# RWKV-7 layers of a four-layer backbone: head-pair keys turned by block transposes and a DRAM exchange instead of identity products

## The chip, the cores and the metric

One core of a Trainium2 chip runs the whole program in one launch. The metric is the device time in microseconds, the median of the runs. The core has TensorE (PE, its weight loads are shown as PEld), VectorE (DVE), ScalarE (ACT), GpSimd (POOL) and SyncE (SP), and each goes through its own instruction list in order. They wait for one another on semaphores.

## The reference, cut to what matters

Four layers over 512 tokens (256 of context, 256 latent) of width 1024. Layers 0 and 3 mix tokens with a bidirectional RWKV-7 recurrence in 16 heads of 64. For each direction and head:

```python
def step(s, inp):
    r_t, w_t, k_t, v_t, kk_t, a_t = inp
    s_kk = jnp.einsum('bhvk,bhk->bhv', s, kk_t)
    s = (s * w_t[:, :, None, :] - s_kk[..., None] * (kk_t * a_t)[:, :, None, :]
         + v_t[..., None] * k_t[:, :, None, :])
    return s, jnp.einsum('bhvk,bhk->bhv', s, r_t)
```

`k_t` is the key that is added, `kk_t * a_t` the one that is taken off. The second direction is the same on flipped tokens, and the context's last state starts the latent part. Layer 1 is Mamba-2, layer 2 attention, and a gated ConvFFN stands after each. The last layer gives no output for the context.

## The kernel before, in words

All data is float32, channels on partitions and tokens along the free dimension, so that two heads fill the 128 partitions (`HALF` names the two halves of 64). The recurrence is done in chunks of 64 tokens (`Q`; there are `NQ` = 8), for eight pairs of heads `i` (`KD`), both directions `d`, written `q = 2 * i + d`.

**The chain.** For each chunk `c` of each `q` there are three dependent steps. W makes a right-hand side from values and state. ACT copies it from PSUM to `WS`. U multiplies by the chunk's inverse matrix `INV`, and DVE copies the result to `US`. S adds `BK` times values and `BK` times `US` to the state (`sp`), makes the outputs, and DVE scales the new state into `STR`. The two directions alternate: W0, W1, U0, U1, S0, S1.

**The work around it.** The order is written out by hand in `slot_steps(h)`. A pair of heads has two slots of 24 chain steps, and each slot has 25 places `k`. At a place the `early` steps are issued, then one chain step, then the `late` steps. Every engine walks the same list and does its own part of each step. While the chain of pair `i - 1` ends and that of pair `i` begins, the lists prepare pairs `i` and `i + 1`, in two halves `s` of four chunks: Gram matrices (`GT`, `R`, `H2`), the inverse (`IB`, `E`, then the levels `Z` and `X`), the decays and keys (`L01` to `sd1`) and the end of pair `i - 1` (`P1` to `P3`). `SD` holds the decayed keys to add, `ADS[i % 2]` those to remove.

**The keys by token.** The `sp` products need both key tensors with tokens on partitions. The step `HB` (`by_token`, four parts in each slot) gets them by multiplying every 64x64 block with the identity `id64` into PSUM bank 7. ACT copies the bank to `BK` (label `bk`).

**The inverse's way through DRAM.** For each half, ACT copies the Gram blocks out (label `n`), SP stores them (`grams_out`, L2499, after a wait at L2496), loads them in blocks of 16 (`blocks_in`, L2507), and POOL inverts them (`block_inverse`). SP stores the result (`inverse_out`, L2514) and loads it back (`inverse_in`, L2522), and DVE expands it at step `E` (`expand`: two products at L3158, transposes at L3162 and L3163). SP does this in order for half 0, then half 1 of each pair. Only the first inverse is DVE's.

Other lines that matter here: L2549 is the helper that issues all these matrix products, L2835 the one for ACT's copies, L3194 the copy to `US`, L3205 the new state, L2946 one ACT instruction of `P2` that comes once for each pair.

## Time and the profile before

| | us |
|---|---|
| median of 3 runs | 3613.45 (3612.48 to 3619.98) |
| the profiled execution | 3610.41 |
| its span, first to last instruction | 3608.6 |
| PE busy | 3447.1 (96%) |
| DVE busy | 2487.9 (69%) |
| ACT busy | 1156.4 (32%) |
| POOL busy | 590.4 (16%) |

The profile is of one execution. Times on rows are in microseconds from the span's start. Busy shares are averages over layers with different limits: the two stretches that the change touches are the chains of layer 0 (about 250 to 665) and of layer 3 (about 2960 to 3342). A matrix product of float32 appears as two records, and neighbouring records overlap, so the pace is read from the distance between starts and not from one record's length.

### The profile page before, as it was taken

Reading aid. Unit: us, or ns where it says so; the run is one execution under the profiler, and the core shown is the slowest. Engines: PE = TensorE matmul, PEld = TensorE weight load, DVE = VectorE, ACT = ScalarE, POOL = GpSimd, SP = SyncE. Lnnn points to the kernel's source line nnn. Section 1 sums busy time; section 2 is a strip of 40 time slices with the busy share of each in tenths; the row PEclk is TensorE's granted clock in tenths of the full one; section 3 lists DMA queues with packets and bytes.
Section 4 is the critical chain, followed back from the end, with each engine's and each line's share of the span. In section 5 each row is a group of like instructions: output and inputs, shape, how many; then the busy total and the mean of one; then the engine's idle time right before and its main releaser. Section 6 shows DMA issues by size and latency. Waiting matters only on the chain. (4 is left out here: it accounts for less than half of the span.)

```text
span 3608.6 us, 74335 instructions
## 1 busy us (share of the span) xinstructions
PE 3447.1 (96%) x28653; PEld 2513.5 (70%) x28653; DVE 2487.9 (69%) x4562; ACT 1156.4 (32%) x2482; POOL 590.4 (16%) x1128
## 2 busy tenths in 40 slices
PE   7998998999999999999999999999999997888999
PEld 2447777688786455555888876678877456777887
DVE  7986665489897657653898954469987956664431
ACT  4035554133202444431233014323310225663210
POOL 1015553000000323320000000000000105553000
PEclk9998999999999999999999999999999998999999
DMA  6641111244353323223444520043434541111454
GB/s 219 207 136 24 21 22 32 74 133 130 118 161 97 105 79 102 82 76 99 129 126 127 162 83 28 25 126 121 136 118 129 170 129 25 25 24 27 134 152 133
DMA packets 584315, 365.07 MB, mean 101 GB/s; under 512 B 126144, under 2 KB 553480, under 8 KB 581928
## 3 DMA queue, kind: packets, MB, share of 16 engines
q1 hardware_dynamic: 557544, 250.40, 25.1%
q0 software_dynamic: 26432, 110.07, 8.7%
q8 instruction: 223, 3.65, 0.4%
q14 instruction: 116, 0.95, 0.1%
HBM read 348.73 MB, written 11.67 MB: 100 GB/s over the span
## 5 line engine op out<-in xcount | busy, mean ns | idle before, releaser
L275 PE MATMUL PS<-H,WR 128*128 128x512 f32 (+1 forms) x1424 | 477.1, 494 | 0.0
L591 DVE SCALAR_TENSOR_TENSOR WORK<-WORK,SC 128x512 f32<-128x512 f32 x616 | 418.3, 746 | 0.7
L275 PEld LDWEIGHTS PS<-H,WR 128*128 128x128 f32 x1424 | 268.0, 190 | 187.3 <-issue 167.2
L2549 PE MATMUL PS<-WORK 64*64 64x64 f32 (+2 forms) x6944 | 361.0, 231 | 29.5 <-ACT BIG L2846 16.6
L571 POOL DMA_DIRECT2D WORK<-in_ada_w_dram x88 | 66.4, 755 | 1857.7 <-DVE WORK L591 839.6
L1474 PE MATMUL PS<-BIG,WR 128*128 128x512 f32 (+1 forms) x944 | 329.4, 503 | 5.2 <-DMA WR<-in_rw_wo_dram 1.7
L2549 PEld LDWEIGHTS PS<-WORK 64*64 64x64 f32 (+1 forms) x6944 | 282.1, 139 | 69.2 <-ACT WORK L2835 23.0
L1474 PEld LDWEIGHTS PS<-BIG,WR 128*128 128x128 f32 x944 | 175.7, 190 | 132.6 <-issue 111.8
L2835 ACT ACTIVATE WORK<-PS 128x64 f32<-128x64 f32 (+3 forms) x528 | 161.4, 326 | 292.0 <-PE PS L2549 286.7
L1012 ACT ACTIVATE WORK<-PS 128x512 f32<-128x512 f32 x252 | 134.7, 541 | 335.6 <-PE PS L945 285.1
L945 PE MATMUL PS<-BIG 128*128 128x256 f32 x984 | 223.9, 380 | 0.0
L275 PE MATMUL PS<-WORK,WR 128*128 128x512 f32 (+1 forms) x544 | 211.7, 545 | 0.9 <-DMA WR<-in_rw_wr_dram 0.9
L945 PEld LDWEIGHTS PS<-BIG 128*128 128x128 f32 x984 | 186.0, 190 | 25.1
L2549 PE MATMUL PS<-BIG,WORK 64*64 64x64 f32 x1920 | 145.7, 228 | 47.0 <-DVE WORK L3194 36.3
L945 PE MATMUL PS<-H,BIG 128*128 128x256 f32 x768 | 177.8, 380 | 0.6 <-ACT H L728 0.4
L945 PE MATMUL PS<-BIG,WORK 128*128 128x256 f32 x792 | 176.3, 379 | 0.0
L1093 DVE SCALAR_TENSOR_TENSOR WORK<-WORK,PV 128x510 f32<-128x510 f32 x252 | 171.7, 743 | 2.6 <-ACT WORK L1023 2.6
L275 PEld LDWEIGHTS PS<-WORK,WR 128*128 128x128 f32 x544 | 102.0, 190 | 101.0 <-issue 88.5
L945 PEld LDWEIGHTS PS<-BIG,WORK 128*128 128x128 f32 x792 | 150.5, 190 | 20.5
L945 PEld LDWEIGHTS PS<-H,BIG 128*128 128x128 f32 x768 | 145.2, 190 | 22.5 <-ACT H L728 3.0
L3009 POOL TENSOR_TENSOR BTN<-BTN,BTP 64x14 f32<-64x14 f32 (+1 forms) x420 | 149.8, 357 | 32.9
L2549 PEld LDWEIGHTS PS<-BIG,WORK 64*64 64x64 f32 x1920 | 100.6, 136 | 74.0 <-DVE WORK L3194 23.4
(363 smaller groups left out, 6391.0 us busy)
## 6 DMA issues: line engine op xcount, KB each, us to landing
WORK<-in_ada_w_dram POOLq DMA_DIRECT2D x88, 1024.0 KB, 6.3
WR<-in_ffn_w_in_dram SPq DMA_DIRECT2D x220, 256.0 KB, 2.9
BIG<-in_ffn_w_in_dram SPq DMA_DIRECT2D x132, 256.0 KB, 3.4
WR<-in_ffn_w_out_dram SPq DMA_DIRECT2D x106, 256.0 KB, 2.8
WR<-in_ssd_w_in_dram SPq DMA_DIRECT2D x96, 256.0 KB, 2.8
BIG<-scratch_dram POOLq DMA_DIRECT2D x8, 2048.0 KB, 7.9
BIG<-in_ffn_w_out_dram SPq DMA_DIRECT2D x36, 256.0 KB, 3.2
BIG<-in_ada_w_dram SPq DMA_DIRECT2D x4, 2048.0 KB, 15.5
```

What stands on the lines that cost most here:

```text
L275: mm = pe.matmul(outs, WR[:, slot, k, 0:m], rhs(k), start=first and k == 0, stop=last and k == nk - 1)
L571: pool.dma_start(AW[:, 2048 * h:2048 * h + 2048].rearrange("p (k c) -> p k c", k=4), rows(a["ada_w"][l])[:, 4 * h:4 * h + 4, n * 512:n * 5 ...
L591: lag(vec.scalar_tensor_tensor(ACC3[:, s_], w, by, ACC3[:, s_], ALU.mult, ALU.add), label)
L945: mm = pe.matmul(out, lhs(k), rhs(k), start=start and k == 0, stop=stop and k == 3)
L1012: s(act.activation(EV[f % 2][:, n0:n0 + n, :], ps[:, 0:n, :], ACT.Copy), lab(f, "e" + bank))
L1093: lag(vec.scalar_tensor_tensor(dst, whole[h][:, :, t // 2:SEG - 1 + t // 2], tap(t, h, f), dst, ALU.mult, ALU.add), lab(f, "cv") if (t, h) ...
L1474: mm = pe.matmul(PS[:, bank, lo:T], WR[:, opened[label], k, :], rhs(8 * r + k), start=r == 0 and k == 0, stop=last and k == nk - 1)
L2549: return pe.matmul(o, lhs, rhs, start=start, stop=stop)
L2835: s(act.activation(dst, src, ACT.Copy), f"{t}.{label}")
L3009: g(pool.tensor_tensor(below, below, product, ALU.add), f"{t}.t{i}.ib{s_}" if j_ == BLK - 2 else None)
```

## The change

The step `HB` is dropped on PE and ACT. A new step `TB` on DVE turns the keys in 32x32 blocks straight from `SD` and `ADS` into `BK`, one instruction for each half `s`, direction `d` and kind `n`, so eight for each pair. A 64x64 turn needs two of the 32-partition blocks exchanged as well. SP does that through a new DRAM tensor: four stores (`swap_out`) and four loads (`swap_in`) for each half, each of 32 partitions by 512 elements (64 KB). The new `BK` interleaves four chunks, so a chunk's keys are read by PE with a step of four elements. `E` and the levels `Z` and `X` move to later places. The copy to `US` of the second direction moves from DVE to ACT. Some waits change with that.

```diff
-        G2, BK, G1R = by_chunk(P), by_chunk(P), by_chunk(Q)
+        G2, G1R = by_chunk(P), by_chunk(Q)
+        BK = work(2 * NQ * P).rearrange("p (s d n a f) -> p s d n a f", s=2, d=2, n=2, a=2)
...
             if s == 0:
-                at = (4, 5, 7, 8, 10, 11, 13, 14) if i else (21, 21, 22, 22, 23, 23, 24, 24)
+                at = (8, 9, 11, 12, 14, 15, 17, 18) if i else (21, 21, 22, 22, 23, 23, 24, 24)
                 early += [(k, *step) for k, step in zip(at, levels)]
-                early += [(1 if i else 20, "E", i, 0), (0, "R", i, 0, 0), (2, "R", i, 0, 1), (9, "H2", both[0], 0),
-                          (12, "HB", both[0], 0, 0), (15, "HB", both[0], 0, 1), (16, "H2", both[1], 0),
-                          (18, "HB", both[1], 0, 0), (20, "HB", both[1], 0, 1)]
+                early += [(5 if i else 20, "E", i, 0), (0, "R", i, 0, 0), (2, "R", i, 0, 1), (9, "H2", both[0], 0),
+                          (16, "H2", both[1], 0)]
+                late += [(k, "TB", i, 0, d, n) for k, (d, n) in zip((0, 1, 2, 3), ((0, 1), (1, 1), (0, 0), (1, 0)))]
...
             else:
-                at = (5, 6, 8, 9, 12, 13, 15, 16)
+                at = (8, 9, 11, 12, 14, 15, 17, 18)
                 early += [(k, *step) for k, step in zip(at, levels)]
-                early += [(2, "E", i, 1), (14, "R", i, 1, 0), (17, "R", i, 1, 1), (2, "H2", both[0], 1),
-                          (3, "HB", both[0], 1, 0), (4, "HB", both[0], 1, 1), (7, "H2", both[1], 1),
-                          (10, "HB", both[1], 1, 0), (11, "HB", both[1], 1, 1)]
+                early += [(5, "E", i, 1), (14, "R", i, 1, 0), (17, "R", i, 1, 1), (2, "H2", both[0], 1),
+                          (7, "H2", both[1], 1)]
+                late += [(k, "TB", i, 1, d, n) for k, (d, n) in zip((0, 1, 4, 6), ((0, 1), (1, 1), (0, 0), (1, 0)))]
...
+            swap = swapped.rearrange("(s b p d n f) -> s b p d n f", s=2, b=4, p=32, d=2, n=2)
+            def swap_out(i, s_):
+                sp.wait_ge(vec_done, C.at(f"{t}.t{i}.tb{s_}"))
+                if i:
+                    sp.wait_ge(swap_loaded, C.at(f"{t}.t{i - 1}.bk{s_}"))
+                for b in range(4):
+                    sp.dma_start(swap[s_, b ^ 1], BK[32 * b:32 * b + 32, s_, :, :, 1 - b % 2, :]).then_inc(
+                        swap_stored, C.mark(swap_stored, f"{t}.t{i}.swap{s_}" if b == 3 else None, 16))
+            def swap_in(i, s_):
+                sp.wait_ge(swap_stored, C.at(f"{t}.t{i}.swap{s_}"))
+                for b in range(4):
+                    sp.dma_start(BK[32 * b:32 * b + 32, s_, :, :, 1 - b % 2, :], swap[s_, b]).then_inc(
+                        swap_loaded, C.mark(swap_loaded, f"{t}.t{i}.bk{s_}" if b == 3 else None, 16))
             for i in range(KD):
                 grams_out(i, 0)
                 blocks_in(i, 0)
                 if i == 0:
                     grams_out(i, 1)
                     blocks_in(i, 1)
+                else:
+                    swap_out(i - 1, 1)
+                    swap_in(i - 1, 1)
                 inverse_out(i, 0)
                 inverse_in(i, 0)
                 if i:
                     grams_out(i, 1)
                     blocks_in(i, 1)
+                swap_out(i, 0)
+                swap_in(i, 0)
                 inverse_out(i, 1)
                 inverse_in(i, 1)
+            swap_out(KD - 1, 1)
+            swap_in(KD - 1, 1)
...
             def vt(n):
-                pe.wait_ge(act_done, C.at(f"{t}.{2 * n - 1}.bk1") if n else C.at(f"{t}.t{n}.a1"))
+                pe.wait_ge(act_done, C.at(f"{t}.t{n}.a1"))
...
                 if c % 4 == 0:
-                    pe.wait_ge(act_done, C.at(f"{t}.{q}.bk{c // 4}"))
-                pe.wait_ge(vec_done, C.at(f"{t}.{q}.us{c}"))
+                    pe.wait_ge(swap_loaded, C.at(f"{t}.t{i}.bk{c // 4}"))
+                by_token = [BK[:, c // 4, d, n].rearrange("p a (f c) -> p (a f) c", c=4)[:, :, ch % 4] for n in range(2)]
+                pe.wait_ge(act_done if d else vec_done, C.at(f"{t}.{q}.us{c}"))
                 if c < NQ - 1:
                     for hs in HALF:
-                        mm(PS[hs, d, P:P + Q], BK[hs, d, c, Q:P], v_tok[hs, tok(ch)], stop=False)
+                        mm(PS[hs, d, P:P + Q], by_token[1][hs], v_tok[hs, tok(ch)], stop=False)
                     for hs in HALF:
-                        last = mm(PS[hs, d, P:P + Q], BK[hs, d, c, 0:Q], US[d][hs, :], start=False)
+                        last = mm(PS[hs, d, P:P + Q], by_token[0][hs], US[d][hs, :], start=False)
...
             def replacement(n, d):
                 act.wait_ge(vec_done, C.at(f"{t}.ka"))
                 if n:
-                    act.wait_ge(pe_done, C.at(f"{t}.{2 * n - 2 + d}.hb1"))
+                    act.wait_ge(pe_done, C.at(f"{t}.{2 * n - 2 + d}.h21"))
+                    act.wait_ge(vec_done, C.at(f"{t}.{2 * n - 2 + d}.turned1"))
...
+            def chain_u(q, c):
+                if q % 2:
+                    act.wait_ge(pe_done, C.at(f"{t}.{q}.u{c}"))
+                    copy(US[1], PS[:, 1, Q:P], f"{q}.us{c}")
...
+            def by_token(i, s_, d, n):
+                half, q = SEGS[s_], 2 * i + d
+                vec_last()
+                if i:
+                    vec.wait_ge(pe_done, C.at(f"{t}.{q - 2}.sp{min(4 * s_ + 3, NQ - 2)}"))
+                src = (SD if n else ADS[i % 2])[:, d, half].rearrange("p (c b t) -> p b c t", b=2, t=32)
+                dst = BK[:, s_, d, n].rearrange("p a (f c) -> p a c f", c=4)
+                lag(vec.transpose(dst, src), f"{t}.{q}.turned{s_}" if n else f"{t}.t{i}.tb{s_}" if d else None)
...
             def chain_u(q, c):
+                if q % 2:
+                    return
                 vec.wait_ge(pe_done, C.at(f"{t}.{q}.u{c}"))
-                lag(vec.tensor_copy(US[q % 2], PS[:, q % 2, Q:P]), f"{t}.{q}.us{c}")
+                lag(vec.tensor_copy(US[0], PS[:, 0, Q:P]), f"{t}.{q}.us{c}")
```

## Rows read from the trace of the kernel before

**Rows 1.** The page: span and PE's busy time.

```profile
span 3608.6 us, 74335 instructions
...
PE 3447.1 (96%) x28653; PEld 2513.5 (70%) x28653; DVE 2487.9 (69%) x4562; ACT 1156.4 (32%) x2482; POOL 590.4 (16%) x1128
```

**Rows 2.** Timeline of ACT, L2946, once a pair: start, length, idle before.

```profile
448.14 0.69 ACT L2946 ACTIVATE WORK<-PS,MC 128x512 f32<-128x512 f32 x1 [0.82 <-PE PS L2549]
...
495.25 0.69 ACT L2946 ACTIVATE WORK<-PS,MC 128x512 f32<-128x512 f32 x1 [0.82 <-PE PS L2549]
...
3149.28 0.47 ACT L2946 ACTIVATE WORK<-PS,MC 128x256 f32<-128x256 f32 x1 [0.40 <-PE PS L2549]
...
3192.46 0.47 ACT L2946 ACTIVATE WORK<-PS,MC 128x256 f32<-128x256 f32 x1 [0.40 <-PE PS L2549]
```

**Rows 3.** Windows, one pair of layer 0: busy by engine, clock, DMA share, GB/s.

```profile
454.00:501.00 47.00, 42.34 (x1104) 36.29 (x1104) 31.48 (x75) 27.74 (x67) 25.07 (x62) 1.00 0.14 23
```

**Rows 4.** Groups by form of PE from 200 to 700, those that read constants.

```profile
L2549 PE MATMUL PS<-K,BIG 64*64 64x64 f32 x1024 | 47.0, 224 | 1.2 <-ACT WORK L2835 1.2
...
L2549 PE MATMUL PS<-K,WORK 64*64 64x64 f32 x256 | 16.6, 218 | 0.0
```

**Rows 5.** Timeline of PE, layer 0, second half of one pair.

```profile
471.82 0.63 PE L2549 MATMUL PS<-K,BIG 64*64 64x64 f32 x16
...
475.87 0.63 PE L2549 MATMUL PS<-K,BIG 64*64 64x64 f32 x16
...
476.45 0.63 PE L2549 MATMUL PS<-K,BIG 64*64 64x64 f32 x16
478.75 0.33 PE L2549 MATMUL PS<-BIG,WORK 64*64 64x64 f32 x4 [1.67 <-DVE WORK L3194]
...
481.98 1.36 PE L2549 MATMUL PS<-WORK 64*64 64x32 f32 x40
483.15 0.66 PE L2549 MATMUL PS<-K,BIG 64*64 64x64 f32 x16
```

**Rows 6.** Timeline of DVE, layer 0, around both steps `E` of one pair.

```profile
454.16 0.45 DVE L3162 STREAM_TRANSPOSE WORK<-WORK 128x256 f32<-128x256 f32 x1
454.53 0.40 DVE L3163 STREAM_TRANSPOSE WORK<-WORK 128x256 f32<-128x256 f32 x1
455.88 0.23 DVE L3194 COPY WORK<-PS 128x64 f32<-128x64 f32 x1 [0.95 <-PE PS L2549]
...
461.59 0.28 DVE L3205 SCALAR_TENSOR_TENSOR WORK<-PS,WORK 128x64 f32<-128x64 f32 x1 [0.67 <-ACT WORK L2835]
...
475.16 1.86 DVE L3158 TENSOR_TENSOR WORK<-WORK,K 128x256 f32<-128x256 f32 x2 [2.12 <-DMA WORK<-blocks_dram]
```

**Rows 7.** Waits of DVE from 310 to 650, then from 3026 to 3285.

```profile
DVE WORK L3158 <- DMA WORK<-blocks_dram: 16.4, 6, 4.7
...
DVE WORK L3158 <- DMA WORK<-blocks_dram: 11.3, 5, 3.4
```

**Rows 8.** Waits of SP's queue, 310 to 650 (two rows), 3026 to 3285.

```profile
SPq L2514 <- POOL BTN L3009: 186.8, 13, 15.3
...
SPq L2496 <- ACT WORK L2835: 22.9, 10, 3.8
...
SPq L2496 <- ACT WORK L2835: 12.6, 6, 3.2
```

**Rows 9.** Timeline of SP, layer 0: issues of one half.

```profile
450.30 2.02 SPq L2499 DMA_DIRECT2D blocks_dram<-WORK  x2
454.20 0.59 SPq L2507 DMA_DIRECT2D BTN<-blocks_dram  x1
469.24 0.47 SPq L2514 DMA_DIRECT2D blocks_dram<-BTN  x1
```

**Rows 10.** DMA issues from 310 to 650: count, size, us to landing.

```profile
blocks_dram<-WORK SPq DMA_DIRECT2D x26, 128.0 KB, 2.5
```

**Rows 11.** Groups by form of ACT from 310 to 650.

```profile
L2835 ACT ACTIVATE WORK<-PS 128x64 f32<-128x64 f32 x116 | 25.6, 221 | 64.5 <-PE PS L2549 63.7
```

More of the change, by code:

```diff
@@ L191, in program @@
         gram_stored = sem("gram_stored")
+        swap_stored = sem("swap_stored")
+        swap_loaded = sem("swap_loaded")
         blocks_loaded = sem("blocks_loaded")
@@ L2489, in rwkv_sp @@
             parts_sp(f"mo{l}", a["rw_wo"][j], [(m, 0) for m in range(2)])
-            wide, narrow = blocks_dram
+            wide, narrow, swapped = blocks_dram
             def grams_out(i, s_):
@@ L2633, in grams_k @@
                 done(last, f"{q}.h2{s}")
-            def by_token(q, s, part_):
-                i, d = q // 2, q % 2
-                if part_:
-                    pass
-                elif d:
-                    pe.wait_ge(act_done, C.at(f"{t}.{q - 1}.bk{s}"))
-                elif s:
-                    pe.wait_ge(act_done, C.at(f"{t}.{q + 1}.bk0"))
-                elif i + 1 < KD:
-                    pe.wait_ge(act_done, C.at(f"{t}.t{i + 1}.a1"))
-                else:
-                    pe.wait_ge(act_done, C.at(f"{t}.t{i}.vt"))
-                for c in (2 * part_, 2 * part_ + 1):
-                    cs = tok(ORDER_Q[d][4 * s + c])
-                    for n, src in enumerate((ADS[i % 2], SD)):
-                        for hs in HALF:
-                            o = slice(c * P + n * Q, c * P + n * Q + Q)
-                            last = mm(PS[hs, 7, o], src[hs, d, cs], half_const("id64")[hs, :])
-                if part_:
-                    done(last, f"{q}.hb{s}")
             def z_step(q, s, m):
@@ L2697, in chain_w @@
                 elif i:
-                    pe.wait_ge(vec_done, C.at(f"{t}.{q - 2}.us{NQ - 1}"))
+                    pe.wait_ge(act_done if d else vec_done, C.at(f"{t}.{q - 2}.us{NQ - 1}"))
                 for hs in HALF:
@@ L2816, in rwkv_pe @@
             pe.wait_ge(act_done, C.at(f"{t}.ve{KD - 1}"))
-            run({**staging, "GT": grams, "R": grams_r, "H2": grams_k, "HB": by_token, "Z": z_step, "X": x_step, "W": chain_w, "U": chain_u, "S": chain_s, "P2": post2, "P3": post3,
+            run({**staging, "GT": grams, "R": grams_r, "H2": grams_k, "Z": z_step, "X": x_step, "W": chain_w, "U": chain_u, "S": chain_s, "P2": post2, "P3": post3,
                  "O": output})
@@ L2908, in first_grams @@
                         grams(n, s_, d)
-            def by_token(q, s_, part_):
-                if part_ == 0:
-                    return
-                act.wait_ge(pe_done, C.at(f"{t}.{q}.hb{s_}"))
-                copy(BK[:, q % 2, 4 * s_:4 * s_ + 4, :].rearrange("p c f -> p (c f)"), PS[:, 7, :], f"{q}.bk{s_}")
             def z_step(q, s_, m):
@@ L2970, in rwkv_act @@
                         stage_first(staging, u)
-            run({**staging, "GT": grams, "HB": by_token, "Z": z_step, "W": chain_w, "S": chain_s, "YE": y_end,
+            run({**staging, "GT": grams, "Z": z_step, "W": chain_w, "U": chain_u, "S": chain_s, "YE": y_end,
                  "P1": post1, "P2": post2, "P2e": post2e})
@@ L3233, in rwkv_vec @@
             run({**staging,
-                 "IB0": first_inverse, "E": expand, "Rv": grams_r, "H2": grams_k, "X": x_step, "U": chain_u, "S": chain_s, "P2v": post2, "P3": post3})
+                 "TB": by_token, "IB0": first_inverse, "E": expand, "Rv": grams_r, "H2": grams_k, "X": x_step, "U": chain_u, "S": chain_s, "P2v": post2, "P3": post3})
             vec_last()
@@ L3382, in build @@
         blocks_dram = [nc.dram_tensor(f"blocks{n}_dram", (size,), F32, kind="Internal").ap()
-                       for n, size in enumerate((16 * BLOCK_STRIDE, P * BLK * BLK))]
+                       for n, size in enumerate((16 * BLOCK_STRIDE, P * BLK * BLK, 2 * P * T))]
         counts = program(nc, args, out, draft, scratch, blocks_dram, **OPTIONS)
```

## Prediction

> **What bounds the kernel now.** The page comes first: the span is 3608.6 us and PE is busy for 96% of it [rows 1]. That share is an average. The change touches only the two chains, so the next thing to read is how fast they go. One instruction of `P2` comes once for each pair of heads. Its starts lie 47.1 us apart in layer 0 and 43.2 us apart in layer 3 [rows 2]. Everything below is in us per pair, and a saving counts 14 times: eight pairs in each of two layers, less the first of each, in whose first slot no chain runs.
>
> The windows of one pair in layer 0 show PE busy for 42.3 of 47, DVE for 31.5, ACT for 27.7 and POOL for 25.1, at a granted clock of 1.00 [rows 3]. PE is the fullest, but it sits idle for 4.7 us, and its records overlap, so its true load is below that. The timeline of PE says where the idle time lies. In the first slot of a pair, from its sixth place or so, product follows product without a gap. Early in the second slot there is a hole of 1.67 us that a DVE copy to `US` ends [rows 5]. The DVE timeline gives the reason: step `E` had waited 2.12 us for the inverse's load, and the copy stood behind it [rows 6]. Such waits sum to 16.4 us in layer 0's stretch of 340 us (7.2 pairs) and 11.3 us in layer 3's of 259 us (6 pairs), so 2.3 and 1.9 us a pair [rows 7].
>
> The waits of SP's queue then show a second loop beside PE. SP stores and loads Gram blocks, waits for POOL's inverse (14.4 us each time), stores and loads it, and goes on to the next half. The only slack in this loop is its wait for ACT's Gram copies: 22.9 us over 7.2 pairs, so 3.2 us a pair in layer 0, and 12.6 over 6, so 2.1, in layer 3 [rows 8]. If nothing else changes in it, this loop can't go round faster than 47.1 - 3.2 = 43.9 and 43.2 - 2.1 = 41.1 us a pair. It caps what the change can bring.
>
> **PE: the identity products.** The constant operands' groups hold 1024 + 256 records in layer 0 [rows 4]. 256 of them are the value turns of `vt` (8 pairs, 16 products, two records each), which stay, so 1024 go: 128 a pair, in eight parts of 16. From 475.87 to 476.45 there are 20 records, 29 ns each [rows 5]. A part is 0.46 us, the eight are 3.7 us a pair. How much of that lies on the path: four parts stand in the gapless stretch of the first slot (the last at 471.82), and one at 483.15 in a full stretch as well. That is 5 x 0.46 = 2.3 us. Two (475.87 and 476.45) fill time ahead of the 1.67 us hole, and one stands ahead of a shorter one. They are hidden now.
>
> **The hole itself.** `E` of the second half moves from place 2 to place 5, three places of some 0.95 us (47.1 / 50), against a wait of 2.12 us [rows 6]. So the load has landed by then, and the copy to `US` doesn't queue behind it. The stretch from 475.75 to 478.75 holds 0.92 us of hidden products and the hole, 3.0 us. With both gone, a chain hop from product to copy to product stays, which can't be under 0.23 us for the copy plus the records at either side, about 0.8. That would give back up to 2.1 us. New turns on DVE stand in the same places, so I take 1.5. Below, it is 0, if the copy is late for another reason.
>
> **DVE.** Eight turns a pair come in. The nearest rows are the transposes of 128x256 at 0.45 and 0.40 us [rows 6], so 3.4 us. Eight copies of 0.21 to 0.23 us leave for ACT, 1.8 us. Net DVE gets 1.6 us more, from 31.5 in 47 to about 33 in 44. In the first slot, the four turns at places 0 to 3 take the room that `E` leaves (1.6 us), and 0.95 and 0.67 us of idle time stand there [rows 6]. But `E` comes back at place 5, behind two scans, and ahead of a new state. I charge 1.2 us of path for all of DVE's changes. The bounds are 0 and the whole 3.4 us.
>
> **ACT** takes eight copies of 221 ns [rows 11], 1.8 us, and loses four of 512 columns, which are longer than two of these each. It is busy for 27.7 of 47 [rows 3]. Zero. Without this cover, a copy behind a long activation would delay its direction by the rest of that activation.
>
> **Z and X** go later in both slots, out of the early places with holes into the full stretch that HB leaves. Their number is unchanged. This is part of why I let only the five exposed parts count, not eight.
>
> **SP and the exchange.** Each half adds eight DMAs. The nearest issue costs 0.59 us, and two larger ones take 2.02 [rows 9], so 4.7 us or, at the dear end, 8.1 us. Between them SP waits for a landing, 2.5 us for 128 KB [rows 10]. All of it lies behind `blocks_in` and ahead of `inverse_out`, where SP does nothing now from 454.8 to 469.2 [rows 9]. The last turn of the first half, place 3, is due near 457.5, so the loads are issued by about 465 (dear: 468), and 1 to 4 us are left. What is queued behind the new waits is `inverse_out`, for which `E` waits. The keys are wanted at place 4 of the next slot, near 477, or 12 us after their load is issued. Zero. The queues carry 23 GB/s at a DMA share of 0.14 [rows 3], and the exchange adds 1 MB a pair, about as much again. The new waits of `replacement` and of the turns name things that are over a slot old or stand earlier in the list.
>
> **The sum.** 2.3 + 1.5 - 1.2 = 2.6 us a pair. In layer 0 that is under the cap of 3.2. In layer 3 SP's loop cuts it to 2.1. Then 7 x 2.6 + 7 x 2.1 = 33 us. The profiled execution took 3610.4 us, 1.8 more than its span and 3.0 less than the median. 3610.4 - 33 + 3.0 = 3580 us. With the bounds of each term (hole 0 to 2.1, DVE 0 to 2.4), this case runs from 3566, where both caps are reached and a little more, to 3594.
>
> **Rivals.**
>
> *Stepped keys are slow to load (slower than before).* PE now reads the keys four elements apart, 16 bytes. No row has such a load. What the rows show is that the load sets the pace of these products: 40 records, most with 32 moving columns, take 1.17 us from 481.98 to 483.15, again 29 ns each, as those with 64 do [rows 5]. So a slower load is seen at once. There are 2 x 2 x 7 pairs of `sp` products with four records each, 112 records a pair of heads. If a stepped load takes twice the time, that is 112 x 29 ns = 3.2 us more, on the chain itself, and 45 us in all: 3580 + 45 = 3625. It decides from 29 + 33 / 14 / 0.112 = 50 ns a record on. Against it: the records with 64 columns might have room that 29 ns does not show. Chance 0.17.
>
> The Trainium skill (SBUF — State Buffer, the paragraph on cachelines in the section on Door 1) speaks here against the change: SBUF has lines of 16 bytes, and an access that crosses to a new line pays unless two or more fall on each. It also calls a stride of four fp32 free, so it can be read both ways for this step. No row here shows it. By its strict reading the sum would be the 3625 of this rival, by the other the 3580 of the forecast. It could slow the turns' writes, too, which have the same step.
>
> *PE's time goes into other waits.* PE is idle for 4.7 us a pair already, and the chain's hops get less cover. If DVE, fuller than before, sets the pace of the early places (its charge is 2.8 and not 1.2), 1.0 us a pair is left: 3613 - 14 = 3599. For it: the copy to `US` ends the hole, and the holes near 455.88 and 461.59. Against it: four parts stood where nothing waited. Chance 0.20.
>
> *The exchange delays the inverse.* If issues cost more than the 1.0 us of the dear row, or the turns come 4 us late, every microsecond past 469.2 goes into SP's loop and takes one off the gain, in both halves. At 1 us each the gain is 0.6 or less: 3605. Chance 0.07.
>
> *All of it comes.* The whole 3.7 us and the hole, held by the caps and a little beyond, if the inverse's own transfers shorten: 3.7 x 14 = 52, so 3561. Chance 0.12. The forecast has 0.44.
>
> **Range and chances.** About 0.2% (7 us) is what a measurement of this kernel can tell from no change. Faster than 3606: the forecast, the full gain, most of the second and half of the third rival, 0.75. Within 7 us: 0.09. Slower: the stepped load, mostly, 0.16. The range from 3560 to 3614 leaves out about 0.05 below and 0.14 above.
>
> **What the next profile should show.** The instruction of `P2` about 44.5 us apart in layer 0 and 41 in layer 3. No constant-reading records but those of `vt`. No wait of `E` for its load in the second slot, and no 1.67 us hole behind it. SP's wait for ACT near zero. Turns of 128x256 at 0.40 to 0.45 us. In S, four records in 0.115 us as now; 0.23 would be the stepped load. SP's wait for POOL down from 14.4 to some 5 us but not gone. I am wrong if `sp` products spread out, if DVE's turns take 0.7 us, if SP's wait for POOL vanishes, or if PE's idle time a pair grows by as much as the products gave.

## The result, and the profile after

| | before | changed |
|---|---|---|
| median, four runs of each on one chip | 3612.97 us | 3678.88 us |
| lowest to highest | 3611.9 to 3619.98 | 3671.03 to 3684.2 |
| the profiled execution | 3610.41 | 3681.47 |

The ratio is 1.0169 (95%: 1.0147 to 1.0192). The kernel became 66 us slower. The forecast was 33 us faster, and its range ended at 3614, so both the sign and the range were wrong.

The page of the changed kernel, the lines that answer to [rows 1]:

```profile
span 3679.7 us, 70679 instructions
PE 3464.7 (94%) x26605; PEld 2526.5 (69%) x26605; DVE 2546.7 (69%) x4562; ACT 1146.5 (31%) x2546; POOL 589.4 (16%) x1128
```

PE has 2048 instructions fewer, as foreseen, and is busy for 17.6 us *longer* than the 3447.1 of before. So the removed time didn't just turn into waits: what PE still does takes longer. The timeline of ACT, the instruction of `P2` once for each pair, as in [rows 2]:

```profile
471.56 0.69 ACT L2952 ACTIVATE WORK<-PS,MC 128x512 f32<-128x512 f32 x1 [0.82 <-PE PS L2575]
524.03 0.69 ACT L2952 ACTIVATE WORK<-PS,MC 128x512 f32<-128x512 f32 x1 [0.82 <-PE PS L2575]
...
3162.65 0.47 ACT L2952 ACTIVATE WORK<-PS,MC 128x256 f32<-128x256 f32 x1 [0.40 <-PE PS L2575]
3210.75 0.47 ACT L2952 ACTIVATE WORK<-PS,MC 128x256 f32<-128x256 f32 x1 [0.39 <-PE PS L2575]
```

A pair takes 52.5 us in layer 0 (47.1 before) and 48.1 in layer 3 (43.2). That is 5.4 and 4.9 more, and seven pairs of each give 72 us, about the whole 71 between the two profiled executions. The place is the one that the prediction looked at. The window of that pair in layer 0, against [rows 3] (columns: the stretch, its length, busy time of PE, PEld, DVE, ACT and POOL, granted clock, DMA share, GB/s):

```profile
471.56:524.03 52.47, 43.73 (x981) 37.41 (x981) 34.89 (x75) 27.21 (x72) 24.65 (x62) 0.97 0.20 40
```

PE has 981 records where it had 1109, and they take 43.7 us instead of 42.5. Its idle time has grown from 4.7 to 8.7 us. DVE has 3.3 us more work, where the prediction counted 1.6. So three things are to be explained: slower PE work, new holes, and more time on DVE.

**Slower PE work.** The timeline of PE in the second slot shows two groups of four records whose successors start late:

```profile
482.04 0.40 PE L2575 MATMUL PS<-BIG,WORK 64*64 64x64 f32 x4
482.27 0.41 PE L2575 MATMUL PS<-WORK 64*64 64x64 f32 x4
482.51 0.29 PE L2575 MATMUL PS<-WORK,BIG 64*64 64x64 f32 x4
482.63 0.29 PE L2575 MATMUL PS<-WORK 64*64 64x64 f32 x4
...
484.88 0.33 PE L2575 MATMUL PS<-BIG,WORK 64*64 64x64 f32 x4 [1.85 <-DVE WORK L3222]
```

From one start to the next it is 0.23, 0.24, and then 0.12 us. The two slow groups are the `sp` products, which read the stepped keys; their neighbours at 0.12 us show that the clock was at its full level. That is the 0.23 which the prediction named as the sign of its first rival. 28 such groups a pair, 0.12 us more each, are 3.4 us. The granted clock of 0.97 over the pair, where it was 1.00, is another 1.6 us at most. Together they are the 5.0 us by which PE's busy time rose from what 128 records less (3.7 us) would have left.

**New holes.** The last line has 1.85 us of idle time that ends with a new state (L3222). DVE's timeline around it:

```profile
482.76 0.69 DVE L3094 TENSOR_TENSOR BIG<-BIG 128x512 f32<-128x512 f32 x1
483.37 1.28 DVE L3090 TENSOR_TENSOR_SCAN BIG<-WORK,BIG 128x512 f32<-128x512 f32 x1
484.57 0.25 DVE L3222 SCALAR_TENSOR_TENSOR WORK<-PS,WORK 128x64 f32<-128x64 f32 x1
...
485.54 0.94 DVE L3173 TENSOR_TENSOR WORK<-WORK,K 128x256 f32<-128x256 f32 x2
486.59 0.45 DVE L3177 STREAM_TRANSPOSE WORK<-WORK 128x256 f32<-128x256 f32 x1
...
487.28 0.24 DVE L3222 SCALAR_TENSOR_TENSOR WORK<-PS,WORK 128x64 f32<-128x64 f32 x1
```

The new state is ready to be made while DVE runs a scan of 1.28 us, and the next one stands behind `E` (L3173 to L3178), which was moved here. Nothing is left on PE's list to fill the time, since `Z` and `X` went later (the runs on the places test this below). PE's waits in a stretch of five pairs, by group of products, show how much there is of this. Before, for the products that start with the keys or the state, and after it the same of the changed kernel (columns: busy us, mean ns, idle before and what ended it):

```profile
L2549 PE MATMUL PS<-BIG,WORK 64*64 64x64 f32 x616 | 46.1, 225 | 10.9 <-DVE WORK L3194 8.0 <-DVE WORK L3205 1.8
```

```profile
L2575 PE MATMUL PS<-BIG,WORK 64*64 64x64 f32 x600 | 53.3, 258 | 29.3 <-DVE WORK L3222 13.9 <-DVE WORK L3226 8.1 <-DVE WORK L3211 7.2
```

The waits for the copy to `US` (L3194, now L3211) hardly fell, from 8.0 to 7.2. The waits for new states went from 1.8 to 22.0 us, 4 us a pair.

**More time on DVE.** The turns, by form, in the changed kernel:

```profile
L3153 DVE STREAM_TRANSPOSE WORK<-BIG 128x256 f32<-128x256 f32 x32 | 20.6, 643 | 3.3 <-DVE WORK L3211 0.4
```

A turn takes 643 ns, not 400 to 450.

### The profile page after: what moved, and what is told of

It is laid out like the page before. It is cut to its first block and busy times, and to the rows that moved or that the text cites. A ratio compares the mean times of both kernels' runs of the same rounds, so it can differ in the third digit from the quotient of the medians.

```text
span 3679.7 us, 70679 instructions
## 1 busy us (share of the span) xinstructions
PE 3464.7 (94%) x26605; PEld 2526.5 (69%) x26605; DVE 2546.7 (69%) x4562; ACT 1146.5 (31%) x2546; POOL 589.4 (16%) x1128
## 5 line engine op out<-in xcount | busy, mean ns | idle before, releaser
L2575 PE MATMUL PS<-WORK 64*64 64x64 f32 (+2 forms) x6944 | 403.9, 246 | 39.5 <-ACT WORK L2841 18.5
L2575 PEld LDWEIGHTS PS<-WORK 64*64 64x64 f32 (+1 forms) x6944 | 326.0, 156 | 70.9 <-ACT WORK L2841 33.7
L2841 ACT ACTIVATE WORK<-PS 128x64 f32<-128x64 f32 (+2 forms) x592 | 148.6, 274 | 360.8 <-PE PS L2575 357.8
L2575 PE MATMUL PS<-BIG,WORK 64*64 64x64 f32 x1920 | 173.0, 260 | 83.8 <-DVE WORK L3222 34.0
L2575 PEld LDWEIGHTS PS<-BIG,WORK 64*64 64x64 f32 x1920 | 125.4, 169 | 131.9 <-DVE WORK L3222 48.8
```

The lines of the kernel that those rows point to most:

```text
L2575: return pe.matmul(o, lhs, rhs, start=start, stop=stop)
L2841: s(act.activation(dst, src, ACT.Copy), f"{t}.{label}")
```

## The experiments

Each run was compared with the kernel before on its own chip. "Distance" is its median less that of the kernel before beside it. By the intervals, a distance is known to some 4 us either way where the kernel ran eight times or more, and to 5 to 8 us where it ran four or five times. A difference between two distances is known less well than either. I count differences under 5 us as nothing.

| run | median | distance | ratio (95%) |
|---|---|---|---|
| changed kernel | 3678.88 | +66 | 1.0169 (1.0147 to 1.0192) |
| after_flat_loads | 3641.35 | +23 | 1.0066 (1.0050 to 1.0083) |
| packed | 3627.42 | +11 | 1.0033 (1.0022 to 1.0044) |
| packed_no_exchange | 3628.83 | +11 | 1.0036 (1.0022 to 1.0051) |
| packed_copy_dve | 3634.55 | +16 | 1.0051 (1.0034 to 1.0067) |
| before_stepped | 3635.2 | +19 | 1.0059 (1.0037 to 1.0082) |
| packed_old_places | 3619.1 | +3 | 1.0007 (0.9995 to 1.0019) |
| packed_old_first | 3602.09 | -12 | 0.9966 (0.9955 to 0.9977) |
| packed_old_second | 3630.24 | +16 | 1.0053 (1.0036 to 1.0070) |
| after_old_first | 3640.84 | +22 | 1.0061 (1.0045 to 1.0078) |
| places_only | 3631.98 | +14 | 1.0044 (1.0027 to 1.0061) |
| places_first | 3629.42 | +15 | 1.0048 (1.0031 to 1.0064) |
| places_second | 3603.75 | -11 | 0.9976 (0.9966 to 0.9986) |
| no_products | 3624.29 | +8 | 1.0023 (1.0013 to 1.0033) |
| no_products_filled | 3610.65 | -5 | 0.9991 (0.9981 to 1.0000) |
| packed_old_filled | 3620.75 | +5 | 1.0016 (1.0006 to 1.0026) |
| packed_old_first_filled | 3615.21 | -4 | 0.9991 (0.9981 to 1.0001) |
| packed_filled | 3663.94 | +48 | 1.0134 (1.0117 to 1.0151) |
| after_filled | 3714.42 | +99 | 1.0278 (1.0261 to 1.0295) |

### The step of four elements

**packed.** The keys lie chunk by chunk: the turns write, and PE reads, adjacent elements. The exchange moves the same bytes in smaller pieces.

```diff
-BK = work(2 * NQ * P).rearrange("p (s d n a f) -> p s d n a f", s=2, d=2, n=2, a=2)
+BK = work(2 * NQ * P).rearrange("p (s d n c a f) -> p s d n c a f", s=2, d=2, n=2, c=4, a=2)
-by_token = [BK[:, c // 4, d, n].rearrange("p a (f c) -> p (a f) c", c=4)[:, :, ch % 4] for n in range(2)]
+by_token = [BK[:, c // 4, d, n, ch % 4].rearrange("p a f -> p (a f)") for n in range(2)]
```

> The changed kernel with the keys laid out chunk by chunk: a turn writes 256 elements side by side and a product's weights are 64 elements side by side; the exchange moves the same bytes in pieces of 128 B instead of 512 B. Theory A (the step of four elements is the loss): the state products go back from 0.24 to 0.115 us for four records, which is 28 groups x 0.12 = 3.4 us a pair of heads, and a turn from 644 to some 400 ns, 8 x 0.24 = 1.9 us of VectorE. Time 3679 - 14 x 3.4 = 3631 if VectorE's part is hidden, 3605 if it is all on the path. Theory B (the new places of E, Z and X and the fuller VectorE make holes, and the granted clock falls behind them): less than 20 us come back, 3660 or more, and the holes of 1.85 and 1.20 us that new-state instructions end stay.

**after_flat_loads.** The changed kernel, but the `sp` products read 64 adjacent zeros of a constant in place of the keys. The turns and the exchange are still made; the keys don't reach the state.

```diff
-by_token = [BK[:, c // 4, d, n].rearrange("p a (f c) -> p (a f) c", c=4)[:, :, ch % 4] for n in range(2)]
+by_token = [{hs: const("blk")[hs, HALF[1 - n]] for n, hs in enumerate(HALF)}] * 2
```

> The changed kernel, in which PE takes the weights of the state products from 64 adjacent zeros of a constant instead of the stepped keys (so real keys do not reach the state; turns, their step, exchange and all waits stay). It splits the 52 us between the changed kernel (3679) and packed (3627) into loads and turns. The stepped load put into the kernel before cost 19 to 21 us. Theory A1: the same 20 us here, so 3658, and the turns (644 for 450 ns) make the other 30. Theory A2: with the identity products gone, the loads are bare in the changed kernel and cost their full 3.4 us a pair: 3679 - 48 = 3631, and the turns' step costs next to nothing.

**before_stepped.** The kernel before, with ACT writing and PE reading its keys with the step.

```diff
+BK = work(2 * NQ * P).rearrange("p (d s n f c) -> p d s n f c", d=2, s=2, n=2, c=4)
-mm(PS[hs, d, P:P + Q], BK[hs, d, c, Q:P], v_tok[hs, tok(ch)], stop=False)
+mm(PS[hs, d, P:P + Q], BK[hs, d, c // 4, 1, :, c % 4], v_tok[hs, tok(ch)], stop=False)
```

> The kernel before with one edit: ACT writes the keys by token with a step of four elements (chunks interleaved, as in the changed kernel) and PE loads them with that step. Nothing else moves. Theory A: each group of four records of the state products takes 0.24 us instead of 0.115, 3.4 us a pair, of which nearly all is on the path, since the products are in the chain: 3613 + 14 x 3.4 = 3661 (3645 if a third is covered). Theory B: the step costs little by itself, under 10 us: at most 3623.

The distance falls from 66 to 23 with flat loads alone and to 11 when the turns' writes are adjacent too. So PE's stepped loads cost 43 us in the changed kernel, 3.1 us a pair, against 3.4 worked out from the starts. What is left to `packed`, about 12, goes with the turns' writes; it is known to some 7 us, and `packed` also changed the order in which the turns read and the size of the exchange's pieces, which no run parts from the writes. In `packed` a turn takes 446 ns, by form:

```profile
L3152 DVE STREAM_TRANSPOSE WORK<-BIG 128x256 f32<-128x256 f32 x29 | 12.9, 446 | 3.0 <-DVE WORK L3210 0.4
```

The timeline of PE in `before_stepped` has the same 0.26 and 0.24 us for the two groups, though nothing else was changed there on PE:

```profile
481.51 0.45 PE L2550 MATMUL PS<-BIG,WORK 64*64 64x64 f32 x4
481.77 0.44 PE L2550 MATMUL PS<-WORK 64*64 64x64 f32 x4
482.01 0.31 PE L2550 MATMUL PS<-WORK,BIG 64*64 64x64 f32 x4
```

But it lost only 19 us there. By group of products over five pairs of layer 0, the hole of [rows 5] had taken up part of it:

```profile
L2550 PE MATMUL PS<-BIG,WORK 64*64 64x64 f32 x598 | 52.2, 251 | 2.6 <-DVE WORK L3195 2.1
```

Idle time ahead of these products is 2.6 us instead of 10.9, so 1.7 us a pair of the 3.4 fell into time that PE had waited anyway. The changed kernel has holes too, but the step doesn't fill them: over five pairs, PE's waits for new states there are 22.0 us with stepped loads and 23.9 with flat ones. So the same step costs 19 us in one list and 43 us in the other.

### The places

**packed_old_places**, **places_only**: all places of `E`, `Z` and `X` put back in `packed`, or all new ones given to the kernel before. **places_first**, **places_second**, **packed_old_first**, **packed_old_second**, **after_old_first**: one slot's alone. The edit of `places_first`:

```diff
-at = (4, 5, 7, 8, 10, 11, 13, 14) if i else (21, 21, 22, 22, 23, 23, 24, 24)
+at = (8, 9, 11, 12, 14, 15, 17, 18) if i else (21, 21, 22, 22, 23, 23, 24, 24)
-early += [(1 if i else 20, "E", i, 0), ...
+early += [(5 if i else 20, "E", i, 0), ...
```

> The packed kernel with E, Z and X at the places that they had before. Theory A has no view of places: within 10 us of packed. Theory B: the places cost, and this one is 20 us or more below packed. Third view, that of the prediction: E at its old place in the second slot waits for its load again, 2.1 us a pair, so 15 to 30 us above packed.

> The kernel before with E, Z and X at the changed kernel's places and nothing else. The prediction held that this takes the 2 us wait of E for its load away, 1.5 us a pair: 3616 - 20 = 3596. Against it stands packed with the old places, 8 us under packed with the new: by that this one is 5 to 15 us slower than before, 3621 to 3631, because E stands behind the scans in the first slot and the levels behind E.

> The kernel before with the new places of E, Z and X in the first slot of each pair only. Both slots together cost 14 to 16 us. In that run's timeline the first slot shows two holes of 1.2 us that new states behind scans and behind E end, where the levels stood before. Theory F (the first slot is it): 10 us or more over before, 3626 or more. Theory S (the second slot): within 5 us of before.

> The kernel before with the new places in the second slot only, where E waited 2 us for its load. If that wait was worth what the prediction said (1.5 us a pair), 3616 - 20 = 3596. Theory F: the wait goes, but a hole behind E of like size comes, so 3606 to 3620. Theory S: 10 us or more over before.

> The packed kernel (3627) with the first slot's places of before and the second slot's new ones: the best combination if the first slot is what costs. Theory F: under packed_old_places (3619), 3605 to 3616. Theory S: about 3627.

> The packed kernel with the second slot's places of before and the first slot's new ones. Theory F: 3627 to 3640. Theory S: 3612 to 3619.

> The changed kernel, stepped keys and all (3679), with only the first slot's E, Z and X at their places of before. If the losses add up, it gains what packed gained from the same edit, 25 us: 3654, and the stepped keys are left with some 50 us. If the stepped turns and the crowded first slot are one loss counted twice, it gains clearly more or less than that: under 3640 or over 3668.

The first slot's new places cost 15 us in the kernel before, 24 in `packed` (from -12 to +11) and 44 in the changed kernel (from +22 to +66). The second slot's gain 11 us in the kernel before and 16 in `packed` with the first slot's old ones (+3 to -12). With the first slot's new places they gain nothing that can be told: `places_only` stands at +14 beside the +15 of `places_first`. The PE timeline of `places_only` has a hole for each of the two late states of the first slot, and one for a late state of the second, where the 1.67 us of before had been:

```profile
464.53 0.33 PE L2549 MATMUL PS<-BIG,WORK 64*64 64x64 f32 x4 [1.18 <-DVE WORK L3205]
...
467.22 0.33 PE L2549 MATMUL PS<-BIG,WORK 64*64 64x64 f32 x4 [1.18 <-DVE WORK L3205]
...
487.24 0.33 PE L2549 MATMUL PS<-BIG,WORK 64*64 64x64 f32 x4 [1.13 <-DVE WORK L3209]
```

The waits of PE in `places_first` say it for five pairs (columns: us in total, times, longest):

```profile
PE PS L2549 <- DVE WORK L3205: 12.3, 11, 1.2
PE PS L2549 <- DVE WORK L3194: 3.9, 10, 0.7
```

12.3 us in 11 waits is 2.5 us a pair for the new states, where the kernel before had 1.8 us in all. There, `Z` and `X` from place 4 on gave PE something to do while DVE ran its scans and `E`.

The same places cost 15, 24 and 44 us, and part of that difference goes with the granted clock. In the windows of layer 0 it is 1.00 in `after_old_first` and 0.94 in the changed kernel:

```profile
330.00:600.00 270.00, 232.37 (x5435) 199.64 (x5432) 188.88 (x409) 148.28 (x393) 142.13 (x345) 1.00 0.21 44
```

```profile
330.00:600.00 270.00, 227.26 (x4990) 194.43 (x4988) 177.44 (x376) 138.05 (x361) 126.89 (x319) 0.94 0.19 39
```

An estimate from the mean clocks of all executions: time below full clock, (1 - clock) x median, is 48 us in the kernel before (0.987), 79 in the changed kernel (0.9785), 52 in `after_old_first` (0.9858), 65 in `packed` (0.9820), 53 in `packed_old_first` (0.9852) and in `places_first` 2 us more than in the kernel before beside it. So the new places of the first slot go with up to 27 us of lost clock in the changed kernel, 12 in `packed` and 2 in the kernel before, which is of the size of what 44 and 24 have over 15. These are upper bounds, since a low clock costs nothing while PE waits, and no run changed the clock alone.

The good half is seen in the DVE timeline of `places_second`. `E` (L3158) starts with no wait for the load, and the two copies to `US` (L3194) have gone ahead of it:

```profile
473.13 0.69 DVE L3177 TENSOR_TENSOR WORK<-PS,K 128x512 f32<-128x512 f32 x1 [3.00 <-PE PS L2549]
473.74 0.35 DVE L3194 COPY WORK<-PS 128x64 f32<-128x64 f32 x2
...
475.64 0.75 DVE L3158 TENSOR_TENSOR WORK<-WORK,K 128x256 f32<-128x256 f32 x2
```

### The identity products

**no_products.** The kernel before without the 128 records a pair and without ACT's copies of them. The keys are zeros set once.

```diff
-"H2": grams_k, "HB": by_token, "Z": z_step, "X": x_step, "W": chain_w
+"H2": grams_k, "Z": z_step, "X": x_step, "W": chain_w
```

> The kernel before without the identity products and ACT's copies of them, and with nothing in their place; the keys by token are zeros for the whole chain, set once, so the state is not updated by real keys. It shows what the removed products were worth alone. By the prediction's count of exposed parts, 2.3 of 3.7 us a pair: 3613 - 14 x 2.3 = 3581. If the products only filled time that PE waits in anyway: 3600 or more. If all of it counts: 3561.

**no_products_filled.** The same with idle products in the second slot, at the places where the identity products stood: 16 of a constant with itself, into a bank that nobody reads.

```diff
+early += [(k, "FL", i, 1, k) for k in (3, 4, 10, 11)]
+def filler(i, s_, part_):
+    for n in range(8):
+        for hs in HALF:
+            mm(PS[hs, 7, n * Q:n * Q + Q], half_const("id64")[hs, :], half_const("id64")[hs, :])
```

> The kernel before without its identity products (keys are zeros, as in the run without products) but with four idle parts at places 3, 4, 10 and 11 of each second slot: 16 products of a constant with itself, which nobody reads. Against no_products (3624) it adds 1.8 us of PE work a pair. Theory C (the products filled the hole in front of the wait of E, and without them the granted clock falls to 0.5 for some 4 to 8 us a pair): the clock stays at 1.00, and the time falls by 8 to 25 us in spite of the added work, to 3599 to 3616. Theory D (the clock is a side effect, the products' time counts where it is): it rises by 14 x 1.8 = 26 at most, 3624 to 3650. If the saved 1.8 us of the first slot are eaten by E's wait for SP and POOL's loop, it ends at the kernel before, 3616, and not below.

`no_products` tests the largest term of the sum. With 3.7 us of work a pair taken off the fullest engine, and nothing put in its place, the kernel is 8 us *slower*. The wait of PE for the copy to `US` over the same five pairs of layer 0, in the kernel before, in `no_products` and in `no_products_filled`:

```profile
PE PS L2549 <- DVE WORK L3194: 9.7, 14, 1.9
```

```profile
PE PS L2549 <- DVE WORK L3192: 20.9, 21, 2.8
```

```profile
PE PS L2550 <- DVE WORK L3199: 3.8, 10, 0.9
```

It grows by 11.2 us, so 2.2 of the 3.7 us a pair only made the hole longer. DVE's timeline of the same slot shows where `E` starts:

```profile
474.70 1.85 DVE L3156 TENSOR_TENSOR WORK<-WORK,K 128x256 f32<-128x256 f32 x2 [2.03 <-PE PS L2549]
```

`E` itself doesn't wait longer than before (2.03 us against 2.12). Counted from the instruction of `P2` that opens the pair (448.36 here, 448.14 before), `E` starts at 26.3 us against 27.0, 0.7 us earlier, and PE falls idle at 27.4 against 28.9, 1.5 us earlier. Of these 1.5, 0.9 are the two hidden parts right ahead of the hole, so the four parts of the first slot brought 0.6 us of their 1.9. PE's timeline, and the windows around it:

```profile
475.34 0.43 PE L2549 MATMUL PS<-WORK 64*64 64x64 f32 x8
...
478.19 0.33 PE L2549 MATMUL PS<-BIG,WORK 64*64 64x64 f32 x4 [2.42 <-DVE WORK L3192]
```

```profile
476.00:480.00 4.00, 1.81 (x42) 1.81 (x43) 3.14 (x8) 0.24 (x2) 0.27 (x1) 0.84 0.31 66
480.00:484.00 4.00, 4.00 (x96) 4.00 (x93) 1.12 (x3) 2.26 (x7) 1.83 (x9) 0.74 0.19 20
```

After an idle stretch of 2.4 us the granted clock falls, and it is below 1.00 in the two windows: part of each was spent at the lower of the two levels, 1.2 GHz. From 480 to 484 PE works without a gap, but from 479.56 on its groups of four records start 0.21 us apart, not 0.12. From the end of the hole to the next `P2` it takes 18.1 us where the kernel before took 16.5, with two parts fewer to do. Over the layers' stretches the mean clock is 0.98 and 0.93 here, and 1.00 and 0.99 before:

```profile
330.00:588.00 258.00, 220.73 (x5396) 186.11 (x5390) 172.78 (x407) 135.09 (x341) 142.40 (x343) 0.98 0.14 23
3067.00:3292.00 225.00, 185.27 (x4284) 157.23 (x4282) 144.51 (x366) 123.52 (x316) 113.74 (x305) 0.93 0.14 23
```

With idle work put back in the second slot alone, 1.8 us a pair, the kernel is 13 us faster than without it. The clock's mean in the same windows is 1.00 in both layers:

```profile
330.00:588.00 258.00, 238.05 (x6186) 204.30 (x6186) 174.09 (x408) 137.05 (x346) 139.86 (x343) 1.00 0.14 24
3067.00:3292.00 225.00, 200.00 (x5237) 172.21 (x5237) 147.36 (x387) 124.18 (x328) 119.60 (x328) 1.00 0.15 25
```

Work that nobody reads can't shorten the chain; the higher clock is the only gain from it that the profiles show. This run also prices the first slot by itself: it has everything of the kernel before but that slot's four parts and ACT's copies, and it is 5 us faster (0.9991, 0.9981 to 1.0000), where four exposed parts would be 1.9 x 14 = 26.

That invites the thought that the changed kernel wants such filling, too. Four runs tested it, with the same idle products at places 4 to 7 of the first slot and 3 to 6 of the second (`after_filled`, `packed_filled`), or at 3 and 4 of the second alone (`packed_old_filled`, `packed_old_first_filled`).

```diff
+early += [(k, "FL", i, 0, k) for k in (4, 5, 6, 7)]
+early += [(k, "FL", i, 1, k) for k in (3, 4, 5, 6)]
```

> The changed kernel, steps and all (3679), with idle parts at places 4 to 7 of the first slot and 3 to 6 of the second, where its PE waits for VectorE's new states. Theory C: the granted clock goes from 0.95 to about 1.00 in the chains, worth up to 0.05 x 50 = 2.5 us a pair, less what the parts overrun the holes: 3650 to 3670. Theory D: 8 x 0.46 = 3.7 us a pair at most on top, up to 3731.

> The packed kernel (3627) with the same idle parts as the run before. Theory C: 3600 to 3620. Theory D: 3627 to 3679.

> The packed kernel with the old places (3619) and two idle parts of 16 products of constants at places 3 and 4 of each second slot. Theory C: the stretches at a clock of 0.5 behind the wait of E go, 1 to 2 us a pair, so 3590 to 3605, faster than the kernel before. Theory D: 3619 to 3632.

> The fastest kernel so far (3602, granted clock 0.984 over the span) with two idle parts of 16 products of constants at places 3 and 4 of each second slot. If the rest of its loss is the clock behind idle stretches of PE: 3585 to 3598. If the holes that matter are elsewhere, or the parts overrun them: 3602 to 3615.

They lost 33 and 37 us, 2 us (no difference) and 9 us. In `after_filled` the clock did come back, to a mean of 0.99 in layer 0:

```profile
340.00:630.00 290.00, 265.94 (x6695) 236.24 (x6694) 186.41 (x397) 142.50 (x381) 133.03 (x331) 0.99 0.20 40
```

against 0.95 in the changed kernel. So the clock alone doesn't explain the changed kernel's loss. The idle work is 3.7 us a pair or 52 us. Of that, 19 and 15 us came back in `after_filled` and `packed_filled`, and the same estimate as above, from mean clocks of 0.9855 and 0.9872, allows the clock 25 and 18. By this reading the filling stood mostly where the chain was waiting for PE; that isn't shown. In `no_products_filled`, two of its four parts stood where PE had nothing else for 2.4 us.

### The exchange and the copy on ACT

**packed_no_exchange.** `packed` without the sixteen DMAs a pair and SP's waits for them; the `sp` products read zeros of a constant.

```diff
-swap_out(i, 0)
-swap_in(i, 0)
```

> The packed kernel without the sixteen exchange transfers of a pair; the state products take zeros of a constant as weights, so unexchanged keys reach nothing. It prices the exchange. The prediction: hidden, so within 4 us of packed (3627). Rival: SP's stores and loads (3.4 and 2.9 us for four) and their traffic delay the inverse: 10 us or more below packed.

**packed_copy_dve.** `packed` with both directions' copies to `US` on DVE.

```diff
-pe.wait_ge(act_done if d else vec_done, C.at(f"{t}.{q}.us{c}"))
+pe.wait_ge(vec_done, C.at(f"{t}.{q}.us{c}"))
```

> The packed kernel with the copy to US of the second direction back on VectorE. If VectorE sets the pace of a pair's first places, 8 copies of 0.21 us more cost up to 1.7 us a pair: 10 to 24 us above packed (3627), so 3637 to 3651. If ScalarE's copies come late behind long activations, it is faster: under 3620.

Without the exchange the distance is the same, +11. It is hidden there, though SP's timeline of the changed kernel shows that its issues were dearer than the nearest row:

```profile
482.16 3.34 SPq L2536 DMA_DIRECT2D blocks_dram<-WORK  x4
...
486.98 2.75 SPq L2542 DMA_DIRECT2D WORK<-blocks_dram  x4
...
493.23 0.50 SPq L2517 DMA_DIRECT2D blocks_dram<-BTN  x1
```

Four stores take 3.3 us to issue and four loads 2.8, so 0.8 and 0.7 us each, between the two prices that the prediction had (0.59 and 1.0). The loads are still issued at 489.7, 3.5 us ahead of `inverse_out`. Whether the exchange is also hidden in `packed_old_first`, the best version, wasn't tried: there `E` waits 6.7 us for its load in the stretch 3026 to 3285, where `packed` has no such wait. The copy on ACT stands at +11 against +16 without it. Their intervals overlap, and 5 us is the edge of what can be told.

### The best version

`packed_old_first` is the changed kernel with adjacent keys and the first slot's places of before. It is 0.34% faster than the kernel before (0.9966, 0.9955 to 0.9977) and 2% faster than the changed one. Its window of one pair of layer 0:

```profile
447.68:493.68 46.00, 39.06 (x981) 32.73 (x981) 33.07 (x75) 27.09 (x72) 24.87 (x62) 1.00 0.28 47
```

PE's busy time did fall, by 3.4 us, from 42.45 to 39.06. But the pair is only 1.1 us shorter, and PE is idle for 6.9 us instead of 4.7. `places_second`, the kernel before with all its identity products and only the second slot's `E`, `Z` and `X` moved, gets 0.9976 (0.9966 to 0.9986). The intervals overlap, and the distances are 2 us apart, which can't be told from nothing. So the removal of the products, the exchange and ACT's copy together are worth little or nothing that these runs can tell, and 11 of the 12 us are had by the second slot's places alone.

## Why the prediction was wrong, step by step

**What bounds the kernel.** "PE is the fullest" was right, and the conclusion from it was not. The 4.7 us of idle time a pair were the sign that in places a chain set the pace: PE to DVE, back to PE, and on. Four parts in a stretch where PE was full brought 5 us of 26 (`no_products_filled`).

**The identity products, 2.3 us.** This step failed as a gain. `no_products` gives -0.6 us a pair (8 us slower) where 2.3 were counted. Three of eight parts were seen to be hidden. What was missed is that a part counted as exposed gives its time to the next wait. PE reaches the hole earlier, the end of `E` comes only a little earlier, and the hole grows (9.7 to 20.9 us over five pairs). The clock falls after that. Why `E` starts only 0.7 us earlier stays open: SP's loop still had slack there, a wait for ACT of 22.9 us over the same five pairs, against 19.6 before.

**The granted clock.** The sum took it as it was in [rows 3], 1.00, also for a kernel with less work on PE. That put a term at nothing without a reason. It was 0.98 and 0.93 in `no_products`, and 0.94 in layer 0 of the changed kernel. By the estimate above, up to 28 us of `no_products` and some 30 of the changed kernel's 66 go with it; these aren't further terms, but a part of those of the places and products.

**The hole, 1.5 us.** The mechanism was right: `E` at place 5 finds its load there. The size was off: 1.5 us a pair would be 21 us, and `places_second` measured 11, so 0.8 a pair.

**`Z`, `X` and `E` in the first slot.** This step failed. "Their number is unchanged" was priced at nothing, and the prediction named "behind two scans, and ahead of a new state" for `E` and charged it to 1.2 us of DVE. The move of the first slot measured 15 us in the kernel before, 24 in `packed`, and 44 in the changed kernel, 1.1, 1.7 and 3.1 us a pair. Steps with no change in number had been the cover for a DVE latency.

**The turns on DVE.** 0.40 to 0.45 us holds where they write adjacent elements (446 ns). With the step they take 643: eight times 0.2 is 1.6 us a pair, and some 12 us were measured.

**Stepped loads.** The rival that had 0.17. Its price of 45 us agrees with the 43 measured, its sign of 0.23 us with the trace, and it was stated before that it would be seen at once. The chance was too low: what spoke against it was only that records with 64 columns might have room, and the row of 29 ns with either 32 or 64 columns spoke for no room. The Trainium skill (SBUF — State Buffer, the paragraph on cachelines in the section on Door 1) asks for two or more accesses on each 16-byte line; the runs agree with that reading, 0.24 against 0.115 us for loads and 643 against 446 ns for the turns. The same paragraph's sentence that a stride of four fp32 is free is contradicted by the same numbers.

**Terms that held.** The exchange is hidden (no difference in `packed_no_exchange`). ACT's copy costs nothing. SP's loop was no cap: its wait for ACT went up to 11.9 us a pair instead of to zero, and its wait for POOL fell from 14.4 to 3.6 us each time, near the 5 that had been foreseen. The waits of SP's queue in the changed kernel, for [rows 8] (layer 0, five pairs):

```profile
SPq L2499 <- ACT WORK L2841: 59.4, 11, 9.9
...
SPq L2517 <- POOL BTN L3015: 36.3, 10, 4.5
```

**The range.** It doesn't follow from the bounds of the terms. Both caps together allow 7 x 5.3 = 37 us, so 3576 and not 3566. The charge for DVE was said to reach 3.4 us and entered with 2.4; with the hole at 0, even 2.4 gives a loss of 0.1 us a pair, so 3615, and 3.4 gives 3629, where the text has 3594. The measured 3679 lies outside that as well.

**The sum, closed with runs.** From the kernel before to the changed one: -12 for the scheme with adjacent keys and the old first slot, +24 for that slot's new places, +12 for the turns' stepped writes, +43 for the stepped loads. The last three were measured one after another on the way from `packed_old_first` to the changed kernel, so they add up to 66 by construction, up to rounding. What is not by construction is that the parts are also there alone: +15 for the places, +19 for the step, and -11 for the second slot. They don't add, since each fills or empties the same holes. In the other order, from `packed_old_first` through `after_old_first`, the step (loads and writes together) costs 34 us and the slot 44.

**Open.** How much of the first slot's 44 us in the changed kernel is DVE's (longer turns at places 0 to 3 ahead of the scans), how much the stepped loads' and how much the clock's wasn't tried apart. Nor was it shown for each filler run why it lost what it did. And the step's write cost in `before_stepped` wasn't parted from its load cost there.

## What to carry to other kernels

Before taking work off a full engine, look at what stands behind each piece: a piece ahead of a wait gives its time to the wait, and here a longer wait cost the clock as well. When an instruction is only moved, name what it had been covering. And look at the innermost step of each operand in a diff, on the reading and on the writing side. A change of layout here outweighed everything that it served, and one edit to make the elements adjacent brought back 55 of 66 us.

## What the runs showed of the hardware

**A step of 16 bytes slows three engines' accesses.** PE's operand loads of 64 columns went from 0.115 to 0.24 us for four records. DVE's block transposes of 128x256 took 446 ns with adjacent writes and 643 with stepped ones (the order of their reads differs as well). ACT's copies out of PSUM, 128x512, have a mean of 593 ns in the kernel before. In `before_stepped`, where those of the keys write with the step, the group is the line below. It still holds others that don't: a single stepped copy takes 1.10 to 1.11 us.

```profile
L2836 ACT ACTIVATE WORK<-PS 128x512 f32<-128x512 f32 x29 | 29.0, 999 | 28.8 <-PE PS L2550 28.8
```

**The granted clock fell after short holes.** In the changed kernel the holes of 1.85 and 1.20 us ahead of 484.88 and 487.58 us are followed, in windows of 2 us, by

```profile
484.00:486.00 2.00, 1.12 (x10) 0.61 (x10) 1.90 (x5) 0.67 (x3) 1.76 (x4) 1.00 0.29 67
486.00:488.00 2.00, 0.80 (x9) 0.42 (x10) 1.79 (x6) 0.69 (x1) 1.61 (x6) 0.85 0.14 33
488.00:490.00 2.00, 2.00 (x44) 2.00 (x42) 0.55 (x2) 1.53 (x4) 1.63 (x5) 0.50 0.27 81
490.00:492.00 2.00, 2.00 (x38) 2.00 (x36) 0.46 (x1) 0.96 (x4) 1.56 (x6) 0.80 0.19 54
```

0.50 is the 1.2 GHz level. PE was already full again while it had it. In the kernel before, the windows from 476 to 484, with its hole of 1.67 us and no second one close behind, stay at 1.00. So some waits of this length are paid a second time, in the work behind them, and others are not.
